# Moving every SBUF buffer of a one-core transformer kernel from multiples of 32 bytes to multiples of 64 bytes

## The chip, the core and the metric

The kernel runs on one core of one Trainium2 chip. The metric is the time of one execution on the device, in microseconds. SBUF is addressed by partition: a tensor of 128 partitions has one start offset in bytes, the same in every partition, and that offset is what this change is about.

## The reference

Two blocks over one sequence of 512 tokens of width 2048, all in float32:

```
# block 1: a linear-attention layer with two branches
proj = x @ w_in                       # 2048 -> 4224 (RWKV7 columns) + 4096 (HGRN2 columns)
o    = concat(rwkv7_scan(...), hgrn2_chunkwise(...))
x    = layer_norm(ALPHA * x + o @ w_out)
# block 2: two attention layers
z = rms_norm(x) @ a_w_in;  q, kv = low_rank(z) ;  x = x + (softmax(q k) v * silu(gate)) @ a_w_out   # 16 heads
z = rms_norm(x) @ b_w_in;  x = x + (norm((softmax(q1 k1) - lam * softmax(q2 k2)) v) * silu(gate)) @ b_w_out  # 8 heads
```

Most of the arithmetic is in the products of the 512-token activations with weight matrices of 2048 rows.

## The kernel before, in words

**Projections.** The activations stand in SBUF transposed: channel on the partition, token along it. A block of 128 channels is `xh[b]` (128 x 512), 16 blocks for 2048 channels. A tile of a projection is 128 output channels x 512 tokens in one PSUM bank `proj[j]`; it sums over 16 blocks. To reach float32 accuracy each operand is split into a high part rounded to `float32r` and the rest (`x_hi`, `x_lo`, `w_hi`, `w_lo`), and each block is three matmuls, `multiply` (L347 to L349): w_hi·x_hi, w_hi·x_lo, w_lo·x_hi. The weights are the stationary operand (128 x 128, loaded into the array by a weight load before each matmul), the activations the moving one, 512 columns. In the rows that follow, `proj<-x_hi,w_hi` names the moving operand first and then the stationary one.

**Weights.** SyncE loads them from HBM in units of 8 blocks (2 DMAs of 256 KB) into the four slots of `raw_weights`; GpSimd splits each unit in four pieces, one TENSOR_SCALAR (L319, to `w_hi`) and one TENSOR_TENSOR (L323, to `w_lo`, which lies over `raw_weights`) per piece; TensorE takes a piece as soon as `w_split` has counted it and gives the slot back through `w_used`.

**Everything else.** The scan, the chunkwise attention, the two softmax attentions, norms and gates run on VectorE and ScalarE with small float32 matmuls on TensorE (banks `work[0..3]`), which are written by hand between the blocks of the next projection: each generator of the mixing work yields how many blocks of projection TensorE runs before its next step. So the order on each engine is fixed in the code; semaphores alone decide when a step starts.

**Placement.** There is no allocator that chooses: an `Arena` hands out offsets one after the other, `take(name, cols)` rounding each size up to a multiple of 32 bytes; `over` lays a second name over an offset. The first arena starts at 16512. Later stages start their own arenas at `stage_start`, `x_start`, `mix2_end` and so on, which are offsets that the first one reached. A few sizes are odd multiples of 32 bytes (`common` has 535 columns, `n_small` 72, `gains` 1), and what is taken behind them is moved by that. Where the buffers stand that this text speaks of:

| buffer | role | start before | modulo 64 | start after | modulo 64 |
|---|---|---|---|---|---|
| common (identity, ones) | moving or stationary | 16512 | 0 | 16512 | 0 |
| raw_weights, w_lo | DMA target, stationary | 20032 | 0 | 20096 | 0 |
| w_hi | stationary | 36416 | 0 | 36480 | 0 |
| x_hi0 (also lat_hi) | moving | 53088 | 32 | 53184 | 0 |
| x_lo0 (also lat_lo) | moving | 69472 | 32 | 69568 | 0 |
| x_hi1, x_lo1 | moving | 85856, 102240 | 32 | 85952, 102336 | 0 |
| mix, o_lo4 | activations, moving | 118624 | 32 | 118720 | 0 |
| o_hi4, y_tokens | moving, output | 151392 | 32 | 151488 | 0 |
| diff_q_lo, diff_q_hi (first of two) | stationary | 184160, 192352 | 32 | 184256, 192448 | 0 |
| diff_k_lo, diff_k_hi (first of two) | moving | 188256, 196448 | 32 | 188352, 196544 | 0 |
| gate_tanh0 | moving once (L1745) | 214944 | 32 | 215104 | 0 |
| diff_rinv_all | read by VectorE | 225536 | 0 | 225664 | 0 |

Of some 160 names, the only buffers of more than 100 columns at a multiple of 64 before are `common`, `raw_weights`, `w_lo`, `w_hi` and `diff_rinv_all`. A block of activations is 2048 bytes long and a block of weights 512, so that the remainder modulo 64 is the same for every block of a buffer.

`keep_warm` (L1535) is the one matmul of 256 or more columns whose two operands both come from `common`: `pe.matmul(bank[:, 0:256], ones, common[:, 0:256])`, in plain float32, which the compiler makes into two MATMUL instructions.

Of the kernel before, what the change touches and what calls it, by code (L numbers as in the profile page):

```python
# [15 lines left out]
P = 128  # L16
# [28 lines left out]
UNIT_KB = 8  # L45
PIECES = 4
PIECE_KB = UNIT_KB // PIECES


U_LORA = 0  # L50
# [118 lines left out]
class Arena:  # L169
# [4 lines left out]

    def take(self, name, cols, dtype=F32):
        t = self.nc.alloc_sbuf_tensor_at(name, [P, cols], dtype, offset=self.at)
        self.at += -(-4 * cols // 32) * 32
        assert self.at <= self.end, (name, self.at - self.end)
        return t

# [24 lines left out]
def build(nc, io):  # L205
    stack = ExitStack()
    with stack:
# [103 lines left out]
        def split_weights(pool):  # L311

            def split(s, unit, turn, pieces=PIECES):
                pool.wait_ge(w_loaded[s], 32 * turn + 32)
                pool.sem_inc(pool_waited, 1)
                part = lambda v, slot, q: v[:, slot, PIECE_KB * q:PIECE_KB * (q + 1)]
                for q in range(pieces + 1):
                    if q < pieces:
                        pool.tensor_scalar(part(hi_v, s, q), part(raw_v, s, q), 1.0, 1.0,  # L319
                                           ALU.mult, ALU.mult).then_inc(hi_done, 1)  # L320
                    if q:
                        pool.wait_ge(hi_done, PIECES * unit + q)
                        pool.tensor_tensor(part(lo_v, s, q - 1), part(raw_v, s, q - 1),  # L323
                                           part(hi_v, s, q - 1).bitcast(F32), ALU.subtract).then_inc(w_split, 1)
                if pieces < PIECES:
                    pool.sem_inc(hi_done, PIECES - pieces)
                    pool.sem_inc(w_split, PIECES - pieces)
# [6 lines left out]
            with turns(U_MLA, U_OUT2) as g:  # L334
                for s in range(SLOTS):
                    split(s, SLOTS * g + s, g, LB // PIECE_KB if s == 1 else PIECES)
            for s in range(SLOTS):
# [7 lines left out]
        def multiply(pe, out, w_h, w_l, a_h, a_l, start, stop):  # L345

            pe.matmul(out, w_h, a_h, start=start, stop=False)  # L347
            pe.matmul(out, w_h, a_l, start=False, stop=False)  # L348
            return pe.matmul(out, w_l, a_h, start=False, stop=stop)  # L349

        def project(pe, unit, tile, bank, slot=0):

            for h in range(2):
# [3 lines left out]
                for k in range(UNIT_KB):  # L357
                    b = h * UNIT_KB + k
                    if k % PIECE_KB == 0:
                        pe.wait_ge(w_split, PIECES * (unit + h) + k // PIECE_KB + 1)  # L360
                    mm = multiply(pe, proj[bank][:, :], hi_v[:, s, k], lo_v[:, s, k], xh[b], xl[b],
# [24 lines left out]
        a1 = Arena(nc, stage_start, nc.sbuf_usable_end)  # L386
        c_rwkv = a1.take("c_rwkv", CR_END)
        lora = a1.take("lora", D_RWKV)
        stage2_start = a1.at
        a1.at = nc.sbuf_usable_end // 32 * 32 - 4 * (2 * P + 64)  # L390
        rows_start = a1.at
        rows1 = a1.take("rows1", P)
        rows2 = a1.take("rows2", P)
# [517 lines left out]
        def rwkv_chunks_act(act, p, prep, take=lambda j: None, behind=lambda: None):  # L911
            need = lambda steps, name: act.wait_ge(steps.sem, steps.done(name, p))
            need(RW_PE, "As")
            act.activation(ask[:, 1:NC_R, 0:64], tokens(work[2][:, 64:512], 64), ACT.Copy).then_inc(RW_ACT.mark("As"), 1)
            run(prep, 1)
            answers = ans.rearrange("p c t -> p (c t)")
            need(RW_PE, "W0")
            act.activation(answers[:, 64:512], work[1][:, 64:512], ACT.Copy).then_inc(RW_ACT.mark("W0"), 1)
            need(RW_PE, "W1")
            act.activation(answers[:, 512:1024], work[2][:, :], ACT.Copy).then_inc(RW_ACT.mark("W1"), 1)  # L920
            take(K_)
            run(prep, 5)
            take(V_)
            run(prep, 2)
            need(RW_DVE, "gcen")
            act.activation(g_sq, g_cen, ACT.Square).then_inc(RW_ACT.mark("gsq"), 1)
            behind()
            need(RW_PE, "back")
            turn_heads(act, g_out, 0, 1).then_inc(RW_ACT.mark("back"), 1)
# [200 lines left out]
        def out_half(pe, st_, i, j, h, ks=range(UNIT_KB)):  # L1130
# [5 lines left out]
            for k in ks:  # L1136
                b = h * UNIT_KB + k
                if k % PIECE_KB == 0 or k == ks[0]:
                    pe.wait_ge(w_split, PIECES * unit + k // PIECE_KB + 1)
                if b < st_.by_pool:  # L1140
# [1598 lines left out]
        def diff_heads_dve(dve, p, before_scores=lambda: None, behind_scores=lambda: None):  # L2739
# [10 lines left out]
            def take_gate(x):  # L2750
                take(6 + x, d_gr[:, :])
                need(DI_ACT, f"t{x}")
                dve.wait_ge(tile_free, T_DIFF + 8 * p + 7 + x)
                done(dve.scalar_tensor_tensor(gate(x), d_gt[:, :], 1.0, d_gr[:, :], ALU.add, ALU.mult), f"gate{x}")
# [222 lines left out]
```

## Time and profile before

| | |
|---|---|
| runs | 3131.08, 3135.16 and 3128.99 us, median 3131.08 |
| profiled execution | span 3133.7 us (the profile gives its span, and no other time for it) |
| TensorE matmul busy | 3095.9 us, 99% of the span |
| TensorE weight load busy | 2480.4 us, 79% |
| GpSimd, VectorE, ScalarE busy | 2076.6, 1531.6 and 803.5 us (66%, 49%, 26%) |
| weights and inputs read | 233.52 MB, 76 GB/s over the span |

Matmuls are pipelined: the duration that a row gives for one (about 395 ns for 512 columns) runs from its start to its modelled end and overlaps the next ones. What a matmul costs in a row of them is the distance between two starts, which the timeline shows.

### The profile page before, as it was taken

The page shows a single profiled execution, that of the slowest core. Times are in us where ns is not written, and L with a number is a line of the kernel's source. Part 1 is how long each engine was busy: PE and PEld are TensorE (multiplying, and loading weights), DVE is VectorE, ACT ScalarE, POOL GpSimd, SP SyncE. Part 2 cuts the span into 40 slices and gives each one's busy share as a digit, 9 for nine tenths or more (in the row PEclk, how much of TensorE's full clock was granted, in tenths as well). Part 3 has the DMA queues.
Part 4 walks back from the last instruction along what each step waited for, and adds up shares of the span by engine and source line. Part 5 has one row for each costly group of instructions (what it writes and reads, how often), then busy time and mean ns, then how long its engine had stood idle before and what let it go on. Part 6 is the DMA issues. An engine that isn't in the chain of part 4 may idle for free.

```text
span 3133.7 us, 60223 instructions
## 1 busy us (share of the span) xinstructions
PE 3095.9 (99%) x19614; PEld 2480.4 (79%) x19614; DVE 1531.6 (49%) x2996; ACT 803.5 (26%) x1552; POOL 2076.6 (66%) x3468
## 2 busy tenths in 40 slices
PE   8999999999999999999999999999999999999999
PEld 7777777788888787788777878888888888878787
DVE  5565555566565766612576773144234324433600
ACT  2333322242332204100355551021112111211300
POOL 7555555488787695887633447886666766666575
PEclk9999999999999999999999999999999999999999
DMA  5222222232222232233211112332222222222142
GB/s 160 62 62 62 62 57 60 62 92 81 74 80 78 77 93 80 81 94 94 71 37 36 44 40 83 94 96 81 81 74 74 80 80 74 74 84 77 54 128 87
DMA packets 461253, 239.61 MB, mean 76 GB/s; under 512 B 27917, under 2 KB 456392, under 8 KB 461128
## 3 DMA queue, kind: packets, MB, share of 16 engines
q1 hardware_dynamic: 457148, 232.14, 25.5%
q10 hardware_dynamic: 3980, 5.63, 0.5%
q8 instruction: 99, 1.62, 0.2%
q14 instruction: 26, 0.21, 0.0%
HBM read 233.52 MB, written 4.19 MB: 76 GB/s over the span
## 4 chain that ended last, share of the span: by engine, by line
PE 91%; DVE 5%; issue 2%; ACT 1%; DMA 0%; POOL 0%; DVEq 0%; ACTq 0%; SPq 0%; PEldq 0%; POOLq 0%
PE proj L347 25%; PE proj L348 24%; PE proj L349 24%; PE work L2612 2%; PE work L2194 2%; PE work L2187 1%; PE work L349 1%; PE work L347 1%; PE work L348 1%; PE work L728 1%; PE work L742 1%; PE work L1306 1%; PE work L1545 1%; PE work L1559 1%; DVE lat_sq L1849 0%
## 5 line engine op out<-in xcount | busy, mean ns | idle before, releaser
L319 POOL TENSOR_SCALAR w_hi<-raw_weights 128x256 fp32r<-128x256 f32 x1728 | 792.3, 468 | 1022.9 <-DMA raw_weights<-w_in 349.5
L323 POOL TENSOR_TENSOR w_lo<-raw_weights,w_hi 128x256 fp32r<-128x256 f32 x1728 | 1357.2, 797 | 0.0
L347 PE MATMUL proj<-x_hi,w_hi 128*128 128x512 f32 x2976 | 1218.4, 409 | 5.8 <-DVE x_lo L1837 3.9
L348 PE MATMUL proj<-x_lo,w_hi 128*128 128x512 f32 x2976 | 1177.1, 396 | 0.0
L349 PE MATMUL proj<-x_hi,w_lo 128*128 128x512 f32 x2976 | 1176.2, 395 | 0.0
L347 PEld LDWEIGHTS proj<-x_hi,w_hi 128*128 128x128 f32 x2976 | 559.8, 188 | 150.3 <-issue 14.2
L349 PEld LDWEIGHTS proj<-x_hi,w_lo 128*128 128x128 f32 x2976 | 558.9, 188 | 136.9
L348 PEld LDWEIGHTS proj<-x_lo,w_hi 128*128 128x128 f32 x2976 | 560.7, 188 | 119.0 <-issue 2.2
L347 PE MATMUL proj<-o_hi,w_hi 128*128 128x512 f32 x253 | 101.8, 402 | 0.4 <-POOL w_lo L323 0.3
L348 PE MATMUL proj<-o_lo,w_hi 128*128 128x512 f32 x253 | 99.9, 395 | 0.0
L349 PE MATMUL proj<-o_hi,w_lo 128*128 128x512 f32 x253 | 99.9, 395 | 0.0
L347 PE MATMUL proj<-lat_hi,w_hi 128*128 128x512 f32 x224 | 93.5, 417 | 2.4 <-DVE mla_q L2281 2.0
L2748 DVE TENSOR_TENSOR diff_v<-proj,diff_rinv_all 128x512 f32<-128x512 f32 x16 | 11.1, 692 | 168.1 <-PE proj L349 168.1
L2677 ACT ACTIVATE diff_exp<-diff_scores,diff_rows,diff_small 128x512 f32<-128x512 f32 x64 | 52.2, 816 | 143.7 <-DVE diff_rows L2809 143.7
L348 PE MATMUL proj<-lat_lo,w_hi 128*128 128x512 f32 x224 | 88.5, 395 | 0.0
L349 PE MATMUL proj<-lat_hi,w_lo 128*128 128x512 f32 x224 | 88.3, 394 | 0.0
L2248 ACT ACTIVATE mla_exp<-mla_scores,mla_rows,mla_small 128x512 f32<-128x512 f32 x64 | 52.1, 815 | 108.7 <-DVE mla_rows L2347 108.7
L2389 DVE TENSOR_TENSOR y_group<-mix,proj 128x512 f32<-128x512 f32 x16 | 11.0, 687 | 139.0 <-PE proj L349 139.0
L2194 PE MATMUL work<-gate_tanh,mla_v_tok 128*128 128x128 f32 x512 | 67.6, 275 | 0.0
L2612 PEld LDWEIGHTS work<-diff_probs_keys,diff_v_tok 128*128 128x128 f32 x512 | 62.0, 191 | 3.0
L2194 PEld LDWEIGHTS work<-gate_tanh,mla_v_tok 128*128 128x128 f32 x512 | 62.8, 192 | 0.7
L2612 PE MATMUL work<-diff_probs_keys,diff_v_tok 128*128 128x128 f32 x512 | 62.3, 275 | 0.0
(497 smaller groups left out, 3930.0 us busy)
## 6 DMA issues: line engine op xcount, KB each, us to landing
raw_weights<-w_in SPq DMA_DIRECT2D x260, 256.0 KB, 3.1
raw_weights<-b_w_in SPq DMA_DIRECT2D x256, 256.0 KB, 3.1
raw_weights<-a_w_in SPq DMA_DIRECT2D x100, 256.0 KB, 3.1
raw_weights<-w_out SPq DMA_DIRECT2D x64, 256.0 KB, 2.9
raw_weights<-a_w_out SPq DMA_DIRECT2D x64, 256.0 KB, 2.9
raw_weights<-b_w_out SPq DMA_DIRECT2D x64, 256.0 KB, 2.9
raw_weights<-a_w_kv_up SPq DMA_DIRECT2D x32, 256.0 KB, 2.7
mix<-x SPq DMA_DIRECT2D x4, 1024.0 KB, 8.7
```

Of the source, the lines that this page charges most:

```text
L319: pool.tensor_scalar(part(hi_v, s, q), part(raw_v, s, q), 1.0, 1.0, ALU.mult, ALU.mult).then_inc(hi_done, 1)
L323: pool.tensor_tensor(part(lo_v, s, q - 1), part(raw_v, s, q - 1), part(hi_v, s, q - 1).bitcast(F32), ALU.subtract).then_inc(w_split, 1)
L347: pe.matmul(out, w_h, a_h, start=start, stop=False)
L348: pe.matmul(out, w_h, a_l, start=False, stop=False)
L349: return pe.matmul(out, w_l, a_h, start=False, stop=stop)
L728: mm = pe.matmul(work[Y_BANKS[q]][HEADS[h ^ 1 ^ q], c64(c)], nb[hs, n, 0], tri[hs, c64(n)], start=True, stop=True)
L742: mm = pe.matmul(work[X_BANKS[q]][hs, c32(c)], y_m[at, c64(NC_H * q + c)], odd if q else tri_over[at, c32(c)], start=True, stop=True)
L1306: mm = pe.matmul(work[2 + n % 2][:, gs], ke[n % 2][:, gs], qe[n % 2][:, gs], start=True, stop=True)
L2194: mm = pe.matmul(work[2 + k % 2][:, 0:P], m_vt[h][:, cs], m_pt[k % 2][:, cs], start=(c == 0), stop=(c == TB - 1))
L2248: act.activation(m_e[k % 2][:, :], m_sc[k % 2][:, :], ACT.Exp, bias=m_row[:, 2 + k % 2:3 + k % 2], scale=m_small[:, k:k + 1], accum_out=m_ ...
L2612: mm = pe.matmul(work[3][:, x * P:(x + 1) * P], d_vt[:, 256 * c + x * P:256 * c + (x + 1) * P], d_pt[:, c * P:(c + 1) * P], start=(c == 0) ...
L2677: act.activation(d_e[c][:, :], d_sc[c][:, :], ACT.Exp, bias=d_row[:, 2 + c:3 + c], scale=d_small[:, 4 * c + k:4 * c + k + 1], accum_out=d_ ...
```

## The change

Each buffer's size is rounded up to a multiple of 64 bytes in place of 32, and the one offset that is counted down from the end of SBUF is rounded down to 64. Since the first arena starts at a multiple of 64, every buffer then does.

```diff
@@ -45,6 +45,7 @@
 UNIT_KB = 8
 PIECES = 4
 PIECE_KB = UNIT_KB // PIECES
+LINE = 64
@@ -174,7 +175,7 @@
     def take(self, name, cols, dtype=F32):
         t = self.nc.alloc_sbuf_tensor_at(name, [P, cols], dtype, offset=self.at)
-        self.at += -(-4 * cols // 32) * 32
+        self.at += -(-4 * cols // LINE) * LINE
         assert self.at <= self.end, (name, self.at - self.end)
         return t
@@ -387,7 +388,7 @@
         stage2_start = a1.at
-        a1.at = nc.sbuf_usable_end // 32 * 32 - 4 * (2 * P + 64)
+        a1.at = nc.sbuf_usable_end // LINE * LINE - 4 * (2 * P + 64)
         rows_start = a1.at
```

The instructions, their order on each engine and their semaphore waits are the same before and after; only addresses differ. The weights move by 64 bytes, the activations and nearly all the rest by 96, some small buffers by up to 224.

## Rows read from the trace of the kernel before

**Rows 1.** The page: busy time, share of the span and instructions by engine; granted clock.
```profile
PE 3095.9 (99%) x19614; PEld 2480.4 (79%) x19614; DVE 1531.6 (49%) x2996; ACT 803.5 (26%) x1552; POOL 2076.6 (66%) x3468
PEclk9999999999999999999999999999999999999999
```
**Rows 2.** The page: the chain that ended last, by engine and by line.
```profile
PE 91%; DVE 5%; issue 2%; ACT 1%; DMA 0%; POOL 0%; DVEq 0%; ACTq 0%; SPq 0%; PEldq 0%; POOLq 0%
```
**Rows 3.** Waits of TensorE: total us, times, longest us.
```profile
PE work L449 <- DMA mix<-x: 8.2, 2, 6.8
PE proj L347 <- DVE x_lo L1837: 3.9, 3, 1.7
PE work L2187 <- DVE mla_probs L2339: 2.6, 5, 0.6
...
PE proj L347 <- POOL w_lo L323: 0.3, 1, 0.3
```
**Rows 4.** Matmul groups by shape: count, busy us, mean ns, idle before.
```profile
L347 PE MATMUL proj<-x_hi,w_hi 128*128 128x512 f32 x2976 | 1218.4, 409 | 5.8 <-DVE x_lo L1837 3.9 <-DVE x_lo L1192 1.8
...
L347 PE MATMUL proj<-o_hi,w_hi 128*128 128x512 f32 x253 | 101.8, 402 | 0.4 <-POOL w_lo L323 0.3
...
L347 PE MATMUL proj<-lat_hi,w_hi 128*128 128x512 f32 x224 | 93.5, 417 | 2.4 <-DVE mla_q L2281 2.0 <-DVE lat_lo L1989 0.3
```
**Rows 5.** Timeline of TensorE in the last stage: start us, duration us; 25 matmuls.
```profile
3012.06 0.40 PE L347 MATMUL proj<-x_hi,w_hi 128*128 128x512 f32 x1
...
3017.66 0.40 PE L347 MATMUL proj<-x_hi,w_hi 128*128 128x512 f32 x1
```
**Rows 6.** Timeline of TensorE from a projection into the scores of differential attention.
```profile
2264.64 0.40 PE L347 MATMUL proj<-x_hi,w_hi 128*128 128x512 f32 x1
...
2266.04 0.39 PE L347 MATMUL work<-diff_k_hi,diff_q_hi 128*128 128x512 f32 x1
2266.26 0.39 PE L348 MATMUL work<-diff_k_lo,diff_q_hi 128*128 128x512 f32 x1
2266.49 0.39 PE L349 MATMUL work<-diff_k_hi,diff_q_lo 128*128 128x512 f32 x1
...
2267.40 0.39 PE L347 MATMUL proj<-x_hi,w_hi 128*128 128x512 f32 x1
```
**Rows 7.** Timeline of TensorE at L1535, and its durations (min/median/max ns).
```profile
1213.30 1.46 PE L1535 MATMUL proj<-common 128*128 128x256 f32 x6
...
L1535 PE MATMUL proj<-common x28: 377/379/634, 1213.3 to 1224.3; 128*128 128x256 f32 x28
```
**Rows 8.** L1745, float32, 512 columns: durations, first and last start us.
```profile
L1745 PE MATMUL work<-gate_tanh,common x2: 590/592/595, 1433.6 to 1434.1; 128*128 128x512 f32 x2
1433.62 1.02 PE L1745 MATMUL work<-gate_tanh,common 128*128 128x512 f32 x2
```
**Rows 9.** Weight loads by shape: mean ns.
```profile
L347 PEld LDWEIGHTS proj<-x_hi,w_hi 128*128 128x128 f32 x2976 | 559.8, 188 | 150.3 <-issue 14.2 <-POOL w_lo L323 9.0 <-DVE x_lo L1837 1.7
...
L347 PEld LDWEIGHTS work<-diff_k_hi,diff_q_hi 128*128 128x128 f32 x64 | 12.0, 188 | 5.5 <-DVE diff_scores L2804 2.9
```
**Rows 10.** The page: two groups of VectorE and the two of GpSimd.
```profile
L2748 DVE TENSOR_TENSOR diff_v<-proj,diff_rinv_all 128x512 f32<-128x512 f32 x16 | 11.1, 692 | 168.1 <-PE proj L349 168.1
L2389 DVE TENSOR_TENSOR y_group<-mix,proj 128x512 f32<-128x512 f32 x16 | 11.0, 687 | 139.0 <-PE proj L349 139.0
...
L319 POOL TENSOR_SCALAR w_hi<-raw_weights 128x256 fp32r<-128x256 f32 x1728 | 792.3, 468 | 1022.9 <-DMA raw_weights<-w_in 349.5
L323 POOL TENSOR_TENSOR w_lo<-raw_weights,w_hi 128x256 fp32r<-128x256 f32 x1728 | 1357.2, 797 | 0.0
```
**Rows 11.** Stretches: length; busy PE, PEld, DVE, ACT, POOL; clock; DMA.
```profile
500.00:1000.00 500.00, 499.24 (x3637) 404.36 (x3636) 307.62 (x625) 162.73 (x329) 369.82 (x565) 1.00 0.26 76
2990.00:3130.00 140.00, 136.87 (x620) 110.67 (x618) 8.25 (x12) 8.98 (x15) 94.64 (x175) 1.00 0.33 101
```

## The prediction

> **What bounds the kernel now.** I read the page first: TensorE is busy 3095.9 of 3133.7 us at the full clock, no other engine over 66% [rows 1], and the chain that ended last lies 91% on TensorE [rows 2]. Then its waits: 8.2 us at the start for the input, the rest in pieces of 4 us or less, 0.3 us for GpSimd's weights [rows 3]. So the end is set by how fast TensorE gets through its own instructions, and an address can matter only if it changes the pace of that engine, or slows another one until TensorE waits for it.
>
> Which instructions: the projections are 2976 + 253 + 224 = 3453 blocks [rows 4] of three matmuls, 10,359 matmuls of 512 columns. Durations overlap, so the pace is read from starts: 24 matmuls between 3012.06 and 3017.66 us [rows 5], 5.60 / 24 = 233.3 ns each. At the 2.4 GHz of the full clock that is 560 columns' time for 512 columns. Together they hold 10,359 x 0.2333 = 2417 us, 77% of the span. All their moving operands (x_hi, x_lo, o, lat) start 32 bytes past a multiple of 64 before, and at a multiple of 64 after; their weights are at a multiple of 64 both times. This is the only cost of the kernel where a few per cent of one kind of instruction is tens of microseconds.
>
> **What the change can cost or save, part by part.**
>
> *Instructions, order, waits, bytes:* none change, 0 us by count.
>
> *Weight loads:* w_hi at remainder 0 takes 188 ns, the scores' stationary operand at remainder 32 also 188 ns [rows 9]. 0 us; besides, a load of 188 ns fits under the 233 ns to the next matmul.
>
> *VectorE and ScalarE:* L2748 reads a tensor at remainder 0 in 692 ns, L2389 works on remainders of 32 alone in 687 ns [rows 10]. That is 5 ns in 690 with the wrong sign for a gain, other operands differing too: 0 us. If VectorE did become 1% slower it would be 15 us of busy time on an engine that is 49% busy [rows 1], of which only the pieces on the 5% of the chain count [rows 2], under 2 us.
>
> *GpSimd and the weight DMAs:* raw_weights, w_hi and w_lo had remainder 0 already. 0 us. The input's DMA goes to `mix`, which moves from 32 to 0; TensorE waits 8.2 us for it [rows 3]. Were each row of 2048 bytes cheaper by one part in 33, that is 0.25 us; I take 0.
>
> *The moving operand of 512 columns:* the one open price. Before, no float32r matmul has a moving operand at a multiple of 64, so it must be bounded. Three places help.
>
> - L1535, both operands in `common` at remainder 0: six in 1.46 us, the last lasting 0.379 us, so (1.46 - 0.379) / 5 = 216 ns between starts [rows 7]. Each is one of two passes of plain float32 over 256 columns, which stream at two cycles a column: 512 cycles are 213.3 ns, and 216 leaves under 3 ns for the change of matmul. The projection's matmul with as many cycles of streaming takes 17.3 ns more.
> - L1745, float32, 512 columns at remainder 32: 1.02 - 0.592 = 0.43 us between its two starts [rows 8], for 1024 cycles = 426.7 ns. At this slower reading rate the offset costs at most a few ns. So what the projections pay is tied to float32r, which asks for twice the bytes per nanosecond (2048 bytes in 233 ns, against 2048 in 430), where a wasted access can't hide.
> - The scores of differential attention, float32r, moving operand at 32 and stationary at 32: six matmuls from 2266.04 to 2267.40 [rows 6], 226.7 ns each, or 544 columns' time, directly behind projection blocks at (2266.04 - 2264.64) / 6 = 233.3. The difference between the two paces is 16 columns' time, and 16 columns of float32 are 64 bytes. So the pace does move with where operands stand or who reads beside it, and it moved by just the time of one 64-byte piece.
>
> A block of 2048 bytes that starts at remainder 32 touches 33 pieces of 64 bytes, one at remainder 0 touches 32. If the reader fetches such pieces, one piece less is 6.67 ns less, 226.7 ns a matmul. Bounds: from +6.67 ns (one piece more, by a conflict) over 0 to -17.3 ns (down to L1535's 216). I take -6.67, since it is the quantum that the trace shows: 10,359 x 6.67 ns = 69 us.
>
> What of it is given back: TensorE's own streams get shorter and VectorE's chains between them do not. Where the mixing work is densest, VectorE is busy 307.6 of 500 us and TensorE idle 0.8 [rows 11], so there is cover, of unknown depth at each single wait. GpSimd needs 4 x (468 + 797) = 5.06 us a unit [rows 10] against 24 x 226.7 = 5.44 us of matmuls (5.60 before), so it stays ahead. In the last stage VectorE is nearly idle [rows 11], so all is kept there. I let 10% go into new waits: 69 - 7 = 62 us.
>
> **Sum.** 3133.7 - 62 = 3071.7 us of span. The profiled execution's span is 2.6 us over the median of the runs, so the median goes to about 3069 us.
>
> [...]
>
> **The rivals.**
>
> *Nothing happens (3131 us).* The 233.3 ns may belong to float32r itself, whatever the address. For it: weight loads and VectorE show no trace of the offset, and the scores that run at 226.7 have their moving operand at remainder 32 too, so something other than that operand's offset makes at least that difference; perhaps the stationary operand, which isn't moved for the projections. Against it: L1535's 216 ns.
>
> *The whole excess goes (about 2970 us).* 10,359 x 17.3 = 179 us. TensorE would then need 24 x 216 = 5.18 us a unit against GpSimd's 5.06, so nearly nothing covers a late piece, and the chains of VectorE show; with 10% lost, 161 us: 3131 - 161 = 2970. For it: L1535. Against: it is plain float32 at the slower reading rate, and the quantum of 16 columns suggests smaller steps.
>
> *Slower (about 3200 us).* The pace may hang on how the moving stream and the next weight load stand to each other, which both read SBUF at once. Before, the projections have them 32 apart modulo 64 and 233.3 ns, the scores 0 apart and 226.7. After, all are 0 apart, but the weights moved by 64 and the activations by 96 bytes, so any pattern coarser than 64 bytes is drawn anew. If this costs one piece more, it is +69 us: 3200. It decides from 0.6 ns a matmul on (10,359 x 0.6 = 6 us). Against it: 24 matmuls over eight blocks and 6 over two others give the same 233.3 ns [rows 5, 6], while each block lies at another address, so a coarse pattern would have to be blind to that.
>
> **How the numbers follow.** One piece less 0.34; nothing 0.33; the whole excess 0.20; slower 0.13. The likeliest gives 3069 us, its own range 3056 to 3085 (from all of 69 us kept to a third lost). The cases of both signs need the wide range: 2965 takes in most of the second rival, 3140 the case of nothing with the spread of the runs; outside are the slower case and the tail of the second rival, under 2 in 10. A measurement can tell about 0.2%, 6 us, from no change: faster 0.54, same 0.33, slower 0.13.
>
> **What will show it.** In the last stage 24 matmuls of a projection take 5.44 us where they took 5.60; the mean duration of L348 and L349 falls with it. Weight loads, GpSimd's pieces and VectorE's groups keep their durations within 1%. TensorE's idle time rises by some microseconds. If the 24 take 5.60 again, the step that fails is that the offset of the moving operand has a price; if 5.2, its size; if over 5.6, the slower rival holds.

## The result, and the profile after

| | before | after |
|---|---|---|
| median | 3131.29 us (4 runs) | 3098.86 us (4 runs, 3097.82 to 3103.98) |
| ratio | | 0.9901, 95% interval 0.9887 to 0.9915 |
| span of the profiled execution | 3133.7 us | 3096.9 us |
| TensorE idle | 31.9 us | 32.9 us |

The change makes the kernel 1.0% faster, 32 us in the medians and 36.8 us between the two profiled executions. The forecast was 62 us.

First the page of the changed kernel: busy time by engine, and the chain by engine.

```profile
span 3096.9 us, 60223 instructions
PE 3058.1 (99%) x19614; PEld 2481.5 (80%) x19614; DVE 1533.8 (50%) x2996; ACT 802.7 (26%) x1552; POOL 2075.4 (67%) x3468
PE 91%; DVE 5%; issue 1%; ACT 1%; DMA 0%; POOL 0%; SPq 0%; DVEq 0%; ACTq 0%; PEldq 0%; POOLq 0%
```

Against [rows 1] and [rows 2]: TensorE's matmul time falls by 37.8 us, all other engines stay within 2.2 us, and the chain is the same but for "issue" (1% where it was 2%). The time came out of TensorE's own stream. Next its matmul groups, its weight loads, and two groups of other engines:

```profile
L348 PE MATMUL proj<-x_hi,w_hi 128*128 128x512 f32 x2976 | 1209.0, 406 | 6.6 <-DVE x_lo L1838 4.2 <-DVE x_lo L1193 2.4
L350 PE MATMUL proj<-x_hi,w_lo 128*128 128x512 f32 x2976 | 1171.2, 394 | 0.0
L349 PE MATMUL proj<-x_lo,w_hi 128*128 128x512 f32 x2976 | 1164.5, 391 | 0.0
...
L348 PEld LDWEIGHTS proj<-x_hi,w_hi 128*128 128x128 f32 x2976 | 560.2, 188 | 138.7 <-POOL w_lo L324 12.8 <-issue 11.5 <-DVE x_lo L1838 2.0
...
L320 POOL TENSOR_SCALAR w_hi<-raw_weights 128x256 fp32r<-128x256 f32 x1728 | 784.0, 462 | 987.9 <-DMA raw_weights<-w_in 340.4
L324 POOL TENSOR_TENSOR w_lo<-raw_weights,w_hi 128x256 fp32r<-128x256 f32 x1728 | 1354.3, 794 | 0.0
L2749 DVE TENSOR_TENSOR diff_v<-proj,diff_rinv_all 128x512 f32<-128x512 f32 x16 | 11.1, 692 | 164.7 <-PE proj L350 164.7
```

A matmul of the first group takes 406 ns where it took 409 [rows 4]. A weight load still takes 188 ns [rows 9], VectorE's group still 692, GpSimd's two 462 and 794 after 468 and 797 [rows 10]; the 462 is 1.3% less, a little more than the 1% that I had allowed. How the pace changed is plainest in the last stage, TensorE's timeline from one matmul to the twenty-fourth behind it:

```profile
3010.01 0.39 PE L348 MATMUL proj<-x_hi,w_hi 128*128 128x512 f32 x1
...
3015.51 0.39 PE L348 MATMUL proj<-x_hi,w_hi 128*128 128x512 f32 x1
```

5.50 us (5.493 before rounding) where it was 5.60 [rows 5]: 228.9 ns a matmul instead of 233.3. The waits of TensorE, total, times and longest:

```profile
PE work L450 <- DMA mix<-x: 10.1, 3, 6.8
PE proj L348 <- DVE x_lo L1838: 4.2, 3, 1.7
PE proj L348 <- DVE mla_q L2282: 2.0, 7, 0.5
```

They are those of before within 2 us [rows 3].

For the experiments I worked out one more number from each trace: the mean distance between the starts of two projection matmuls that follow one another in less than 250 ns (9,271 to 9,284 such distances in each trace), and, apart from it, what is left between TensorE's first and last start when these are taken out. TensorE's idle time counts from the start of the span.

| | mean distance | the rest | TensorE idle |
|---|---|---|---|
| before | 233.21 ns | 957.7 us | 31.9 us |
| after | 229.38 ns | 955.1 us | 32.9 us |

These distances sum to 2163.0 us before and 2128.9 us after, 34.1 us less, and the rest is 2.6 us less; together they are the 36.8 us of the span. So a faster pace of the projections tells nearly all of the saving, and nothing to speak of was lost in new waits. What sets the pace is the question.

### The profile page after: what moved, and what is told of

It is laid out like the page before. It is cut to its first block, busy times and chain, and to the rows that moved or that the text cites. A ratio compares the mean times of both kernels' runs of the same rounds, so it can differ in the third digit from the quotient of the medians.

```text
span 3096.9 us, 60223 instructions
## 1 busy us (share of the span) xinstructions
PE 3058.1 (99%) x19614; PEld 2481.5 (80%) x19614; DVE 1533.8 (50%) x2996; ACT 802.7 (26%) x1552; POOL 2075.4 (67%) x3468
## 4 chain that ended last, share of the span: by engine, by line
PE 91%; DVE 5%; issue 1%; ACT 1%; DMA 0%; POOL 0%; SPq 0%; DVEq 0%; ACTq 0%; PEldq 0%; POOLq 0%
PE proj L348 25%; PE proj L350 24%; PE proj L349 24%; PE work L2613 2%; PE work L2195 2%; PE work L2188 1%; PE work L348 1%; PE work L349 1%; PE work L350 1%; PE work L729 1%; PE work L743 1%; PE work L1307 1%; PE work L1560 1%; PE work L1546 1%; DVE lat_sq L1850 0%
## 5 line engine op out<-in xcount | busy, mean ns | idle before, releaser
L320 POOL TENSOR_SCALAR w_hi<-raw_weights 128x256 fp32r<-128x256 f32 x1728 | 784.0, 462 | 987.9 <-DMA raw_weights<-w_in 340.4
L349 PE MATMUL proj<-x_lo,w_hi 128*128 128x512 f32 x2976 | 1164.5, 391 | 0.0
```

## The experiments

The offset that I forecast by was that of the moving operand modulo 64. But the change moves the weights too, by 64 bytes, and the activations by 96. Call D the offset of the moving block less that of the weights. Before, w_hi begins at byte 36416 and the moving block at 53088: D = 16672, or 288 modulo 512. After, D is 320 modulo 512. Weight blocks lie 512 bytes apart and moving blocks 2048, so D modulo 512 is the same for every pair of blocks. The scores of attention have both operands at the same place modulo 512, D = 0, and they are the ones that ran at 226.7 ns [rows 6].

### 1. Matmuls alone, at chosen offsets

The kernel leaves out the whole computation: it fills one buffer and runs series of 72 projection-like matmuls (w_hi by x_hi, w_hi by x_lo, w_lo by x_hi), each series with its own shifts in bytes (w_hi, w_lo, x_hi, x_lo, in this order in the call). Nothing else runs beside them.

```diff
+            for a, s in series(1, "std", 0, 0, 0, 0): mm = pe.matmul(*a, **s)  # a
+            for a, s in series(2, "std", 64, 64, 96, 96): mm = pe.matmul(*a, **s)  # b
+            for a, s in series(3, "std", 0, 0, 32, 32): mm = pe.matmul(*a, **s)  # c
+            for a, s in series(4, "std", 32, 32, 0, 0): mm = pe.matmul(*a, **s)  # d
+            for a, s in series(5, "std", 32, 32, 32, 32): mm = pe.matmul(*a, **s)  # e
...
```

> This kernel leaves out the whole computation: it fills SBUF with one block of the input and runs series of 72 matmuls, three per block as in the projections, at chosen offsets; every series stands on a line of its own. Measured is the distance of two starts in each series. Theory A (the moving operand's own offset modulo 64): 233.3 ns where it starts at remainder 32, 228.9 at remainder 0, whatever the weights' offset (the series with the weights alone shifted by 32 stays at 233.3, the one with both shifted by 32 gives 228.9). Theory B (the relation of the moving stream and the weight load modulo 64): 228.9 where both have the same remainder (weights alone shifted by 32, activations alone shifted by 32, the offsets of after), 233.3 where they differ (the offsets of before, both shifted by 32). Theory C (a coarser pattern): shifts of the activations by 32, 96 and 160 give different paces. Float32 at the two offsets: 434 ns or less at both by A and B.

Each row gives durations (min/median/max) and the first and last start of a series, 71 distances apart; L263 has the offsets of before, L264 of after, L265 moves the activations by 32, L266 the weights, L267 both, and L286 and L287 are plain float32 (two passes each) at the offsets of before and with the activations moved by 32, which is the D of after:

```profile
L263 PE MATMUL proj<-field x72: 393/396/400, 46.9 to 63.5; 128*128 128x512 f32 x72
L264 PE MATMUL proj<-field x72: 388/392/396, 63.7 to 80.0; 128*128 128x512 f32 x72
L265 PE MATMUL proj<-field x72: 388/392/399, 80.2 to 96.5; 128*128 128x512 f32 x72
L266 PE MATMUL proj<-field x72: 389/389/397, 96.7 to 112.8; 128*128 128x512 f32 x72
L267 PE MATMUL proj<-field x72: 393/396/399, 113.1 to 129.6; 128*128 128x512 f32 x72
...
L286 PE MATMUL proj<-field x144: 590/592/593, 413.0 to 474.4; 128*128 128x512 f32 x144
L287 PE MATMUL proj<-field x144: 592/592/592, 474.8 to 536.2; 128*128 128x512 f32 x144
```

Steady paces, from the unrounded starts of the second half of each series: 233.4, 229.0, 228.9, 226.7 and 233.3 ns. The series reproduces the kernel's two paces from the offsets alone, without any other engine. L266 leaves the moving operand 32 past a multiple of 64 and is the fastest; L267 brings it to a multiple of 64 and is as slow as before. So its remainder alone is not the cause, and one 64-byte piece less is not what was saved. L263 and L267 have the same D, and so have L264 and L265. Float32 takes 429.2 ns a pass in both series: it doesn't notice. A shift of only x_hi or only x_lo by 32 gives 231.1 ns, between the two. Three matmuls in a row on the same pair, or all 72 on one pair of blocks, keep the two paces as well (233.3 ns at the D of before, 228.8 at that of after), so neither the change between high and low parts nor the walk over the blocks is needed.

### 2. The kernel before with only the activations moved, or only the weights

```diff
# act_by_32, against the kernel before: the activations and all behind them 32 bytes on (D = 320)
         n_small = fixed.take("n_small", 72)
+        fixed.at += 32
         x_start = fixed.at
# weights_at_32, against the kernel before: n_small taken ahead of the weights, activations unmoved (D = 0)
+        n_small = fixed.take("n_small", 72)
         weights_at = fixed.at
...
-        n_small = fixed.take("n_small", 72)
```

> The kernel before with 32 bytes left free ahead of the activations, so that activations and all behind them stand at multiples of 64, by 32 bytes further on and not 96; weights and the small tables ahead of them as before. Theories A and B: the whole gain, 3095 to 3103 us, 24 projection matmuls in 5.49 us. Theory C: another pace than 228.9 ns, so a time off by 10 us or more. If the small tables mattered: near 3131.

> The kernel before with n_small taken ahead of the weights, so that the weights stand at remainder 32 modulo 64 and the activations, unmoved, too. Theory A (the moving operand alone): no change, 3128 to 3135 us, 5.60 us for 24 matmuls. Theory B (equal remainders of moving and stationary operand): the gain comes without moving the activations, 3095 to 3105 us, 5.49 us or less.

`n_small` has 288 bytes. Taken ahead of the weights it moves them by 288, w_hi to 36704, and D is 53088 - 36704 = 16384, 0 modulo 512. The expectations of this run's repetition (section 4) and of the sweep in section 3 have D = 256 for it; modulo 256 that is the same.

| | multiples of | D mod 512 | median | ratio to before | mean distance | rest | idle |
|---|---|---|---|---|---|---|---|
| act_by_32 | 64 for the big buffers | 320 | 3097.4 us | 0.9886 [0.9869, 0.9904] | 229.35 ns | 954.7 us | 34.3 us |
| weights_at_32 | 32, none of the operands at 64 | 0 | 3082.9 us | 0.9842 [0.9823, 0.9860] | 227.91 ns | 954.4 us | 34.1 us |

Both traces in the last stage, first act_by_32, 5.49 us for 24 matmuls:

```profile
3009.84 0.39 PE L348 MATMUL proj<-x_hi,w_hi 128*128 128x512 f32 x1
...
3015.33 0.39 PE L348 MATMUL proj<-x_hi,w_hi 128*128 128x512 f32 x1
```

and weights_at_32, 5.44 us, 226.7 ns each:

```profile
3000.26 0.39 PE L347 MATMUL proj<-x_hi,w_hi 128*128 128x512 f32 x1
...
3005.70 0.39 PE L347 MATMUL proj<-x_hi,w_hi 128*128 128x512 f32 x1
```

act_by_32 is the change's whole effect from one padding of 32 bytes: that the change also aligned the small tables and the row buffers did nothing that can be told. weights_at_32 has both operands of every projection 32 past a multiple of 64, the remainder that the change does away with, and is 16 us faster than the changed kernel.

### 3. D in steps of 16 bytes

The same series, with the computation left out again; the weights stay, the activations move.

```diff
+            for a, s in series(1, "std", 0, 0, -288, -288): mm = pe.matmul(*a, **s)  # D=0
+            for a, s in series(3, "std", 0, 0, -256, -256): mm = pe.matmul(*a, **s)  # D=32
+            for a, s in series(5, "std", 0, 0, -224, -224): mm = pe.matmul(*a, **s)  # D=64
...
+            for a, s in series(40, "std", 0, 0, 1888, 1888): mm = pe.matmul(*a, **s)  # D=2176
```

> Leaves out the whole computation: only series of matmuls, as in the first sweep. D is the offset of the moving block less that of the weights, so 288 modulo 512 for the projections before, 320 after, 256 with the weights at remainder 32. Theory D (the distance of the two reads of SBUF modulo 256 sets the pace): 226.7 ns at D = 0, 256, 512, 768, 1024, 2048; 228.9 at 64, 320, 1088; 233.3 at 32, 288, 544, 1056, 128, 384, 2176, and the same value at each D and D + 256. Theory A (the moving operand's offset alone) has one value for all D that are 32 modulo 64 and has already failed on the first sweep; if D and D + 256 differ, the period is longer. Of two series in which weights and activations alternate between places 32 bytes apart, the one whose matmuls stand 256 from the weights of the next matmul is at 226.7 ns if the conflict is with the weight load that runs meanwhile, the one whose matmuls stand 256 from their own weights if it is not.

The rows of D = 0 (L273), 32 (L275), 64 (L277), 128 (L281), 256 (L289) and 320 (L293):

```profile
L273 PE MATMUL proj<-field x72: 387/389/402, 46.7 to 62.8; 128*128 128x512 f32 x72
L275 PE MATMUL proj<-field x72: 393/396/399, 79.7 to 96.3; 128*128 128x512 f32 x72
L277 PE MATMUL proj<-field x72: 388/392/397, 113.3 to 129.6; 128*128 128x512 f32 x72
L281 PE MATMUL proj<-field x72: 390/393/404, 179.9 to 196.4; 128*128 128x512 f32 x72
L289 PE MATMUL proj<-field x72: 387/389/397, 313.8 to 329.9; 128*128 128x512 f32 x72
L293 PE MATMUL proj<-field x72: 387/392/397, 380.4 to 396.7; 128*128 128x512 f32 x72
```

Steady pace, ns, worked out from the starts of the second half of each series:

| D | 0 | 16 | 32 | 48 | 64 | 80 | 96 | 112 |
|---|---|---|---|---|---|---|---|---|
| ns | 226.7 | 231.6 | 233.3 | 233.4 | 228.8 | 231.1 | 233.2 | 231.3 |

| D | 128 | 144 | 160 | 176 | 192 | 208 | 224 | 240 |
|---|---|---|---|---|---|---|---|---|
| ns | 232.4 | 233.3 | 234.3 | 231.1 | 233.3 | 234.7 | 233.4 | 226.7 |

All sixteen values come again at D + 256; 512, 768, 1024 and 2048 give 226.7, 544 and 1056 give 233.3, and 1088 gives 228.8. So the pace of these matmuls follows D modulo 256. Only at D = 128 did something else tell as well: 232.4 here, also at D = 384, but 233.5 in the first sweep at D = 384, with every operand at the same place, and at D = 2176. D = 4, 8, 12 and 36 give 238.1, 232.7, 228.9 and 235.4. No offset tried goes below 226.7 ns, which is 544 columns' time at the 0.417 ns a column of section 5.

The single distances show that the pace is a pattern into which the series settles. At D = 0 (L273) the first seven are 241, 224, 231, 236, 228, 232 and 231 ns, and from the eighth on all are 226 or 227. At D = 64 they go 226, 229, 232 over and over, at D = 32 in groups of four between 230 and 235. At D = 384 the same offsets have settled into two patterns: in this sweep one of eight or nine between 228 and 241 (232.4 in the mean), in the first one of 229 and 238 in turn (233.5). Those two series differ only in what ran before them and in the chip. So D = 128 has not one price but two, and what chooses between them is not shown.

Two more series were to tell whether the stream meets the load of its own weights or of those behind it. With a matmul's own weights at D = 256 and the next matmul's off it, 231.6 ns; the other way round, 230.0. Neither gives 226.7, so this decided nothing.

### 4. The changed kernel, all at multiples of 64, with a larger gap

```diff
# after_plus_64, against the changed kernel: D = 384, which is 128 modulo 256
         n_small = fixed.take("n_small", 72)
+        fixed.at += 64
         x_start = fixed.at
# after_plus_192, against the changed kernel: D = 512, which is 0 modulo 512
+        fixed.at += 192
```

> The changed kernel with 64 more bytes left free ahead of the activations: every buffer still at a multiple of 64, distance D = 384 modulo 512 (128 modulo 256) in the projections. Theory D: the first sweep has 233.4 ns at this distance, so all of the gain is gone, 3128 to 3136 us. Theory A (multiples of 64 are what helps): no change against the changed kernel, 3095 to 3104 us.

> The changed kernel with 192 more bytes ahead of the activations: all at multiples of 64, D = 0 modulo 512 (320 + 192). Theory D: 226.7 ns a matmul, the time of the kernel with the weights at remainder 32, 3080 to 3088 us. Theory A: 3095 to 3104 us as the changed kernel.

after_plus_64 took 3124.7 us (10 runs), ratio 0.9975 [0.9965, 0.9986]; mean distance 232.32 ns, rest 952.8 us, idle 31.2 us. In the last stage 24 matmuls took 5.57 us:

```profile
3011.88 0.40 PE L349 MATMUL proj<-x_hi,w_hi 128*128 128x512 f32 x1
...
3017.45 0.39 PE L349 MATMUL proj<-x_hi,w_hi 128*128 128x512 f32 x1
```

Every buffer is at a multiple of 64 as in the changed kernel, and three quarters of the gain are gone. It came out 3 us under my expectation, which had priced D = 128 by the first sweep (233.4 ns); 232.32 ns is near the other of the two patterns.

after_plus_192 took 3091.7 us with a wide spread (3086.74 to 3101.77, 4 runs), ratio 0.9874 [0.9845, 0.9902], though its mean distance was nearly that of weights_at_32, 227.96 ns. I ran it again beside the other two good placings, on one chip:

> The changed kernel once more, beside the next two on one chip: distance D = 320 (64 modulo 256) in the projections, 228.9 ns a matmul in long runs. 3096 to 3103 us.

> The kernel before with n_small ahead of the weights: D = 256, all large buffers at remainder 32 modulo 64. 226.7 ns, 3081 to 3086 us. If the distance is all that counts, the next kernel has the same time within 3 us.

> The changed kernel with 192 more bytes ahead of the activations: D = 512, all at multiples of 64. By the distance alone the time of the kernel just before, 3081 to 3087 us; if multiples of 64 help or harm beside the distance, another by more than 3 us.

| same chip; before 3132.32 us | median | ratio to before | mean distance | idle |
|---|---|---|---|---|
| the changed kernel | 3100.67 us | 0.9898 [0.9883, 0.9913] | 229.38 ns | 34.1 us |
| weights_at_32 (offsets 32 mod 64, D = 0) | 3083.85 us | 0.9852 [0.9836, 0.9868] | 227.93 ns | 33.2 us |
| after_plus_192 (offsets 0 mod 64, D = 512) | 3083.73 us | 0.9846 [0.9833, 0.9860] | 227.96 ns | 33.7 us |

The last one again shows 24 matmuls in 5.44 us:

```profile
2999.68 0.39 PE L349 MATMUL proj<-x_hi,w_hi 128*128 128x512 f32 x1
...
3005.12 0.39 PE L349 MATMUL proj<-x_hi,w_hi 128*128 128x512 f32 x1
```

With D a multiple of 512 in both, 64-byte alignment is worth nothing: 0.1 us between the two. No full kernel had D = 256 modulo 512; that 256 is as good rests on the sweeps. Both beat the changed kernel by 17 us (0.5%) and the one before by 1.5%.

### 5. Fewer columns of weights, fewer moving columns

If what the stream loses were a collision with a weight load in proportion to how long the load is, then fewer weight columns should shrink the loss. The computation is left out here too.

```diff
# against the kernel of section 3
-                        yield (proj[n % 4][:, 0:cols], w, x), dict(start=i == 0, stop=i == total - 1)
+                        yield (proj[n % 4][0:m, 0:cols], w[:, 0:m], x), dict(start=i == 0, stop=i == total - 1)
...
+            for a, s in series(4, "cols32", 0, 0, -288, -288): mm = pe.matmul(*a, **s)  # 32 weight columns, D=0
```

> Leaves out the whole computation: series of matmuls as in the sweeps before, now with fewer weight columns (96, 64, 32 of 128) and with fewer moving columns. Without any conflict 512 columns would take 213.3 ns and a few more. Theory E (the other party is the weight load of the next matmul, which reads SBUF while this one streams): fewer weight columns, less conflict; at D = 32 from 233.3 ns for 128 columns to about 225 for 64 and 221 for 32, at D = 0 from 226.7 to 221 and 218; where loads of 128 and 32 columns alternate, the distances of starts alternate too. Theory F (the moving stream of float32r is slow by itself and the weights only set its phase): the same pace at every number of weight columns. Float32 stays at 429.2 ns a pass at D = 0 and 32 by both. With fewer moving columns the excess over the columns' own time falls in proportion under F and stays the same in ns under E until the weight load is the longer.

| weight columns | 128 | 96 | 64 | 32 |
|---|---|---|---|---|
| D = 0 | 226.7 | 230.0 | 229.8 | 231.7 |
| D = 32 | 233.3 | 226.7 | 230.7 | 226.7 |
| D = 64 | 228.8 | 233.4 | 228.4 | 231.3 |
| D = 128 | 232.4 | 231.7 | 229.3 | 230.7 |

Three rows of matmuls, D = 0 with 128 columns (L278), D = 32 with 128 (L282) and with 32 columns (L285), and the weight loads of D = 0 with 128 and with 32 columns (L278, L281), 188 and 108 ns:

```profile
L278 PE MATMUL proj<-field x72: 389/389/398, 46.2 to 62.3; 128*128 128x512 f32 x72
...
L282 PE MATMUL proj<-field x72: 389/394/397, 112.3 to 128.9; 128*128 128x512 f32 x72
...
L285 PE MATMUL proj<-field x72: 389/389/396, 162.0 to 178.1; 128*32 128x512 f32 x72
...
L278 PEld LDWEIGHTS proj<-field x72: 187/188/188, 45.9 to 62.1; 128*128 128x128 f32 x72
...
L281 PEld LDWEIGHTS proj<-field x72: 107/108/112, 95.4 to 111.9; 128*32 128x32 f32 x72
```

The idea in this form fell: the load got 80 ns shorter, and yet at D = 0 fewer columns make it slower, at D = 32 faster. Which D is good changes with the number of weight columns, and none of the sixteen series is below 226.7 ns. One series of the same run speaks for a part of the load all the same: with 128 and 32 weight columns in turn at D = 0, the distance behind a start is 229.0 ns where the load of 32 columns is the next one and 231.0 where that of 128 is. That is the direction of the idea, at 2 ns, but both are slower than 128 columns alone. With 448, 384, 320 and 256 moving columns the distances are 202.7, 173.3, 146.7 and 120.0 ns at D = 0 and 206.7, 176.7, 146.6 and 117.8 at D = 32: the offset matters from 384 columns up by 3 to 7 ns, and at 256 the order turns round. At D = 0 the distance grows from 120.0 to 226.7 ns for 256 columns more, 0.417 ns a column at a granted clock of 1.00, or 2.4 columns a ns; the 2.4 GHz and the cycles of the prediction are counted at this rate, one cycle for one such column. What a matmul takes beyond its own columns is 13.3 ns, or 32 columns' time, at D = 0 for 256, 320, 384 and 512 columns alike (16.0 ns at 448): in these series a fixed price of each matmul and no share of its columns. The 213.3 ns that the expectation gives 512 columns without a conflict are an estimate, 512 times 0.417 ns; no float32r series of 512 columns ran under 226.7 ns.

## Where the prediction was right and where it failed

**What bounds the kernel:** right. TensorE's matmul time fell by 37.8 us and the span by 36.8, with the chain and the waits as they were.

**The terms at zero** (instructions, weight loads, VectorE, GpSimd, the input's DMA): right, each within 1.3% (GpSimd's 468 to 462 ns the largest), none of them on the path. act_by_32, with the tables unmoved, has the time of the changed kernel.

**The moving operand of 512 columns** is the step that failed, in cause and in size; that the time fell at all was luck. I put "one piece less is 6.67 ns less", 69 us, on the remainder of the moving operand modulo 64. Measured are 3.83 ns in the mean (4.4 in long runs), 40 us over the same 10,359 matmuls, of which the span shows 36.8; and what the pace follows is D, which the change happened to take from 32 to 64 modulo 256. Two runs show it: weights_at_32 gains more without any operand at a multiple of 64, and after_plus_64 has every operand there and gains 0.25%. Nor is 6.67 ns a smallest step: the sweep has paces at 228.8, 231.1, 232.4 and 234.7 ns too. The 6.67 ns that I read from the scores [rows 6] are real, 233.3 to 226.7, but they are the price between D = 32 and D = 0, and the six matmuls of those rows are the good stretch of the scores (all distances between scores under 250 ns have a mean of 228.7). I had even written that the scores' moving operand stood at remainder 32 like the projections', and that their stationary operand stood elsewhere; that row alone excluded a reader of 64-byte pieces that looks at the moving operand only. The sum would have needed a pace at D = 64, and no row of the kernel before had one. That float32r pays because it asks for more bytes per nanosecond was my guess; the sweeps show that plain float32 keeps its 429.2 ns a pass, not why.

**10% given back in new waits:** wrong too, by far less. TensorE's idle time rose by 1 us, and by no more than 2.4 us in any other variant. In weights_at_32 the mean distance fell by 5.30 ns, 55 us over 10,359 matmuls, and the span by 51.3 us. What falls short of the full 6.67 ns is elsewhere: a stretch of projections behind another matmul starts slow. Its first three distances are 231.5 to 232.1 ns in the mean, and only from about the eleventh on they are 226.7; half of the 580 stretches have at most four distances. From 100 to 500 us the mean distance of weights_at_32 is 230.3 ns, from 3000 us on 226.7; before, 232.8 and 233.3.

**A slip in the range:** "all of 69 us kept" is 3131 - 69 = 3062 us and not 3056.

**The rivals.** "Nothing happens" had the right reason against me, that "something other than that operand's offset" made the scores fast, and was wrong that this something stood still. "The whole excess goes" rested on L1535 [rows 7]: that is plain float32, which for 512 columns runs at 429.2 ns a pass at all four distances tried (D = 0, 32, 288 and 320), so its 216 ns say nothing on float32r; no float32r series of 512 columns came below 226.7. The slower rival named the true quantity, how the moving stream and the weights stand to each other, and drew its sign wrongly. Its objection, that blocks at different addresses all run at 233.3 ns, was no objection: they are 512 and 2048 bytes apart, multiples of the pattern's 256.

**Open.** That the pace follows D modulo 256 is shown for 512 moving and 128 weight columns; why it does is not. The collision priced by the length of the load fell, own or next weights were not told apart, no run explains the fixed 13.3 ns, and with 192 moving columns the distance is 111.6 or 111.7 ns at D = 32 and 0, 18 ns over the 93.3 that 0.417 a column and 13.3 would give; what sets it is not shown.

## What to carry to other kernels

For float32r matmuls of 512 columns with 128 columns of fresh weights each, look at the distance between the two operands' offsets, not at their alignment: place moving and stationary blocks a multiple of 256 bytes apart, which gave 226.7 ns at all six such distances of section 3 where others gave up to 238.1, and keep their strides multiples of 256 (here 512 and 2048). With fewer columns on either side another distance can be the good one (section 5). Here a padding of 192 bytes was worth 0.5% on top of the change, and the change itself worked because it happened to move that distance. The full pace of 226.7 ns came only in long stretches of equal matmuls: in weights_at_32 the first three distances of a stretch had 231.5 to 232.1 ns in the mean, and half of the stretches have no more than four. Measure such a price in a short series of matmuls by distances between starts, one offset at a time, with the stationary operand moved in one series as well; and use a fast neighbour in the profile as evidence only after writing down everything in which it differs.

## What the runs showed of the hardware

- A float32r matmul of 512 columns with 128 columns of weights had a pace between 226.7 and 238.1 ns in the series, at a granted clock of 1.00, set by the distance between its operands modulo 256 and, at D = 128 (232.4 or 233.5), by something besides; the slowest found is D = 4. The pace is a settled pattern of distances, reached in section 3's series at D = 0 after seven of them.
- At D = 0, from 256 to 512 columns, each moving column of float32r takes 0.417 ns in the mean, and a matmul of 256, 320, 384 or 512 columns takes 13.3 ns beyond them (one of 448, 16.0).
- Plain float32 takes 429.2 ns a pass of 512 columns at D = 0, 32, 288 and 320, and 216 ns one of 256 columns at L1535 [rows 7]: 0.833 ns a column, two of float32r's columns, and 2.5 ns besides, where float32r at D = 0 takes 13.3.
- The load of 128 weight columns lasts 188 ns at the offsets of before and of after, in weights_at_32's too: the loss shows in the distance between matmuls alone. Loads of 96, 64 and 32 columns last 161, 134 and 108 ns.
